# Ordering a split block's 24 products as three sweeps over its eight tiles

## The reference

```
h = rms_norm(x, g)          # [256, 1024]
proj = h @ w_in             # weights 1024 x (some thousands)
...
x = x + m @ w_out
```

## Time and profile before

| | |
|---|---|
| median of 3 runs | 1797.45 us (1797.22 to 1798.41) |
| the profiled execution | 1802.54 us |
| its span, first to last instruction | 1800.7 us |
| TensorE busy | 93% of the span |
| VectorE busy | 55% |
| ScalarE busy | 36% |
| TensorE's mean granted clock | 0.947 of full |

### The profile page before, as it was taken

The page is one execution under the profiler, slowest core; times in us unless marked ns, Lnnn a source line. Parts: engine busy times, 40 slices in busy tenths (PEclk is TensorE's granted clock), DMA queues, the critical chain, the costliest instruction groups (busy, mean ns, idle before and its releaser), DMA issues. The chain is left out here.

```text
span 1800.7 us, 29177 instructions
## 1 busy us (share of the span) xinstructions
PE 1676.3 (93%) x11890; PEld 1530.6 (85%) x11890; DVE 988.1 (55%) x1658; ACT 651.5 (36%) x899; POOL 12.5 (1%) x16
## 2 busy tenths in 40 slices
PE   7989999889998999989878999999999978988998
PEld 6788889889998889889878998899899868986677
DVE  6798554755556689564644334434433435456534
ACT  4542435344444543335332222222222224245321
POOL 1000000000000000000000000000000000000000
PEclk9999999999998999999987999999999988789899
DMA  7432233445553442222333878887788754422122
GB/s 276 150 105 76 79 106 103 140 133 188 187 193 129 141 140 94 71 100 89 116 107 119 292 268 276 273 291 267 278 280 283 277 204 145 157 79 79 59 71 82
DMA packets 82034, 292.72 MB, mean 163 GB/s; under 512 B 9095, under 2 KB 11647, under 8 KB 81679
## 3 DMA queue, kind: packets, MB, share of 16 engines
q1 hardware_dynamic: 81791, 290.10, 47.0%
q10 hardware_dynamic: 144, 1.24, 0.2%
HBM read 290.22 MB, written 1.08 MB: 162 GB/s over the span
## 5 line engine op out<-in xcount | busy, mean ns | idle before, releaser
L266 PE MATMUL bank_P<-h_hi,weights_hi 128*128 128x256 f32 x1584 | 475.1, 300 | 37.7 <-DVE h_lo L1069 18.9
L268 PE MATMUL bank_P<-h_hi,ring_lo 128*128 128x256 f32 x1584 | 458.2, 289 | 0.0
L267 PE MATMUL bank_P<-h_lo,weights_hi 128*128 128x256 f32 x1584 | 457.7, 289 | 0.0
L371 DVE TENSOR_TENSOR ring_lo<-ring,weights_hi 128x1024 fp32r<-128x1024 f32 x245 | 298.3, 1224 | 260.3 <-ACT weights_hi L352 257.6
L266 PEld LDWEIGHTS bank_P<-h_hi,weights_hi 128*128 128x128 f32 x1584 | 311.6, 197 | 54.5 <-issue 26.9
L352 ACT ACTIVATE weights_hi<-ring 128x1024 fp32r<-128x1024 f32 x245 | 257.2, 1058 | 221.1 <-PE bank_P L268 183.6
L268 PEld LDWEIGHTS bank_P<-h_hi,ring_lo 128*128 128x128 f32 x1584 | 315.9, 199 | 0.0
L267 PEld LDWEIGHTS bank_P<-h_lo,weights_hi 128*128 128x128 f32 x1584 | 312.6, 197 | 1.7 <-issue 1.0
L1507 PEld LDWEIGHTS bank_P<-arena,ring 128*128 128x128 f32 x2048 | 238.2, 193 | 7.3 <-issue 1.6
L1507 PE MATMUL bank_P<-arena,ring 128*128 x2048 | 238.6, 276 | 1.3 <-DVE arena L1621 1.3
L1647 DVE TENSOR_TENSOR arena<-arena,bank_P 128x96 f32<-128x96 f32 x64 | 16.3, 254 | 170.2 <-ACT arena L1553 170.2
(11 more groups left out here) (403 smaller groups left out, 2400.3 us busy)
## 6 DMA issues: line engine op xcount, KB each, us to landing
ring<-stream SPq DMA_DIRECT2D x541, 512.0 KB, 3.9
cst<-consts SPq DMA_DIRECT2D x1, 1712.0 KB, 10.5
arena<-params ACTq DMA_DIRECT2D x1, 1211.0 KB, 7.1
arena<-x SPq DMA_DIRECT2D x1, 1024.0 KB, 5.1
arena<-bias_vec SPq DMA_DIRECT2D x8, 128.0 KB
out<-arena SPq DMA_DIRECT2D x2, 512.0 KB
arena<-params SPq DMA_DIRECT2D x2, 256.0 KB, 7.6
arena<-bias_vec SPq DMA_DIRECT2D x8, 64.0 KB
```

The source lines that it names most:

```text
L266: pe.matmul(out, hi, x_hi, start=start, stop=False, skip_group_check=True)
L267: pe.matmul(out, hi, x_lo, start=False, stop=False, skip_group_check=True)
L268: return pe.matmul(out, lo, x_hi, start=False, stop=stop, skip_group_check=True)
L371: v.tensor_tensor(env["ring_lo"][:, slot, :], env["ring"][:, slot, :], env["w_hi"][:, i % HIS, :].bitcast(F32), ALU.subtract).then_inc(sel ...
```

## The change

The products of a block are no longer made tile by tile. A new method `sweeps` makes high x high for all eight tiles, then high x low activation for all eight, then low x high activation for all eight. TensorE waits for the high part ahead of the first sweep and for the low part ahead of the third. Where the activation is new, it waits for `h_hi_q` in the first sweep and for `h_lo_q` in the second. The block before is released with the first matmul instead of the third. In the scan of the mixer section, where a block's matmuls are dealt out between other products, they are still dealt out three at a time. The five places that call it are alike; one of them is shown.

```diff
+    def sweeps(self, out, x_hi, x_lo, hi_ready=None, lo_ready=None):
+        slot, part = (self.first + self.n) % RING, self.splits % HIS
+        self.n += 1
+        self.splits += 1
+        hi = self.env["w_hi"][:, part, :].rearrange("p (k n) -> p k n", k=KD)
+        lo = self.env["ring_lo"][:, slot, :].rearrange("p (k n) -> p k n", k=KD)
+        pe = self.pe
+        pe.wait_ge(self.env["sem"]("blocks_hi_parts_written"), self.splits)
+        for k in range(KD):
+            if hi_ready and k % 2 == 0:
+                pe.wait_ge(*self.env["after"](*hi_ready(k // 2)))
+            o, start = out(k)
+            mm = pe.matmul(o, hi[:, k, :], x_hi(k), start=start, stop=False, skip_group_check=True)
+            if k == 0:
+                self.release(mm)
+                self.unreleased += 1
+            yield mm
+        for k in range(KD):
+            if lo_ready and k % 2 == 0:
+                pe.wait_ge(*self.env["after"](*lo_ready(k // 2)))
+            yield pe.matmul(out(k)[0], hi[:, k, :], x_lo(k), start=False, stop=False, skip_group_check=True)
+        pe.wait_ge(self.env["sem"]("blocks_lo_parts_written"), self.splits)
+        for k in range(KD):
+            yield pe.matmul(out(k)[0], lo[:, k, :], x_hi(k), start=False, stop=(k == KD - 1), skip_group_check=True)
...
         def project(bank, j, name=None):
 
-            hi, lo = blocks.split()
-            for k in range(KD):
-                if blocks.n == 1 and k % 2 == 0:
-                    pe.wait_ge(*after(f"h_lo_{k // 2}"))
-                mm = three_passes(pe, bank[:, j * T:(j + 1) * T], hi[:, k, :], lo[:, k, :], h_hi[:, k, :], h_lo[:, k, :],
-                                  k == 0, k == KD - 1)
-                if k == 0:
-                    blocks.release(mm)
-            blocks.unreleased += 1
+            waits = (lambda q: (f"h_hi_{q}",), lambda q: (f"h_lo_{q}",)) if blocks.n == 0 else ()
+            for mm in blocks.sweeps(lambda k: (bank[:, j * T:(j + 1) * T], k == 0), lambda k: h_hi[:, k, :], lambda k: h_lo[:, k, :],
+                                    *waits):
+                pass
             return mm
```

More of the change, by code:

```diff
@@ L807, in gate_stream @@
                 bank = bank_of[turn[0] % 2]
[L808 to L819 removed]
+                out = bank[:, (n % 2) * T:(n % 2 + 1) * T]
+                for i, mm in enumerate(blocks.sweeps(lambda k: (out, k == 0), lambda k: h_hi[:, k, :], lambda k: h_lo[:, k, :])):
+                    if i == 3 * KD - 1 and n % 2:
+                        turn[0] += 1
+                        mm.then_inc(*done("pe", f"p_gate_{n // 2}"))
+                    if i % 3 == 2:
+                        yield
         stream = gate_stream()
@@ L861, in tensor @@
             for j in range(2):
-                hi, lo = blocks.split()
-                for k in range(KD):
-                    if q + j == 0 and k % 2 == 0:
-                        pe.wait_ge(*after(f"m_lo_{k // 2}"))
-                    mm = three_passes(pe, bank[:, j * T:(j + 1) * T], hi[:, k, :], lo[:, k, :], h_hi[:, k, :], h_lo[:, k, :],
-                                      k == 0, k == KD - 1)
-                    if k == 0:
-                        blocks.release(mm)
-                blocks.unreleased += 1
+                waits = (lambda i: (f"m_hi_{i}",), lambda i: (f"m_lo_{i}",)) if q + j == 0 else ()
+                for mm in blocks.sweeps(lambda k: (bank[:, j * T:(j + 1) * T], k == 0), lambda k: h_hi[:, k, :],
+                                        lambda k: h_lo[:, k, :], *waits):
+                    pass
             mm.then_inc(*done("pe", f"p_x_{q}"))
@@ L1695, in up @@
             for i in range(2):
-                hi, lo = blocks.split()
-                for k in range(KD):
-                    if f + i == 0 and k % 2 == 0:
-                        pe.wait_ge(*after(f"h2_lo_{k // 2}", "mix0"))
-                    mm = three_passes(pe, bank[:, i * T:(i + 1) * T], hi[:, k, :], lo[:, k, :], h_hi[:, k, :], h_lo[:, k, :],
-                                      k == 0, k == KD - 1)
-                    if k == 0:
-                        blocks.release(mm)
-                blocks.unreleased += 1
+                waits = (lambda q: (f"h2_hi_{q}", "mix0"), lambda q: (f"h2_lo_{q}", "mix0")) if f + i == 0 else ()
+                for mm in blocks.sweeps(lambda k: (bank[:, i * T:(i + 1) * T], k == 0), lambda k: h_hi[:, k, :],
+                                        lambda k: h_lo[:, k, :], *waits):
+                    pass
             mm.then_inc(*done("pe", f"tile_{f}"))
@@ L1956, in tile @@
         def tile(bank, j, waits=None):
-            hi, lo = blocks.split()
-            for k in range(KD):
-                if waits and k % 2 == 0:
-                    pe.wait_ge(*after(f"{waits}_{k // 2}"))
-                mm = three_passes(pe, bank[:, j * T:(j + 1) * T], hi[:, k, :], lo[:, k, :], h_hi[:, k, :], h_lo[:, k, :],
-                                  k == 0, k == KD - 1)
-                if k == 0:
-                    blocks.release(mm)
-            blocks.unreleased += 1
+            ready = (lambda q: (f"{waits}_hi_{q}",), lambda q: (f"{waits}_lo_{q}",)) if waits else ()
+            for mm in blocks.sweeps(lambda k: (bank[:, j * T:(j + 1) * T], k == 0), lambda k: h_hi[:, k, :], lambda k: h_lo[:, k, :],
+                                    *ready):
+                pass
             return mm
@@ L1990, in big @@
             mm.then_inc(*done("pe", name))
-        big("p_kvc", "vc_raw", (lambda b, j: tile(b, j, "h_lo"), tile))
+        big("p_kvc", "vc_raw", (lambda b, j: tile(b, j, "h"), tile))
         big("p_q0", "q0", (tile, tile))
@@ L2173, in tensor @@
         for i in range(4):
[L2174 removed]
+            big(f"p_x_{i}", f"x_{i}", (lambda b, j: tile(b, j, None if i else "m"), tile))
         for a in range(TT2):
```

13 lines of the change are left out of this document (removed).

## The result

The changed kernel took 1804.62 us in the median of 11 runs (1798.97 to 1808.48), the kernel before 1798.23 us in 11 runs on the same chip (1794.68 to 1801.62): a ratio of 1.0034, 95% interval 1.0022 to 1.0045, or 6.1 us more. A second set of 10 runs gave 1804.91 us and 1.0032 (1.0017 to 1.0046). The change made the kernel slower by a third of a per cent. The forecast was 1800.2 us in a range of 1795 to 1806, so the time lies in the range, but 4.4 us above the forecast, outside the forecast's own narrower range of 1797 to 1801, and nearer to rival (c) at 1806.

What follows compares the result with a forecast made beforehand. TensorE, busy for 93% of the span, was taken as the bound. Terms -5.1 + 5.9 + 2.0 = +2.8 us on 1797.45 us gave 1800.2 us; range 1795 to 1806, the forecast's own 1797 to 1801.

Steps and rivals of the forecast that it cites:

- rival (c): In the mixers' m blocks the clock falls behind a longer stop: +8.8 us, 1806 us, slower; chance 0.34.
- late wait at `conv_b`: At the first conv_b block, only DVE's wait for swap_q is won, in both layers: -5.1 us.
- h blocks: Four h blocks: six more matmuls behind the last high quarter, clock returning later in two: +5.9 us.
- m blocks: Three m blocks: six more matmuls behind the last high quarter, 0.65 us each: +2.0 us.
- distance inside a block: Matmuls inside a block were taken to stay 0.12 us apart at full clock; no cost counted.
- release with the first matmul: Release of the block before comes 0.24 us earlier and could hurry ACT's next high part; counted at nothing.
- the part that had 0.35: Chance given to the whole kernel being slower by over 0.2% (3.6 us).
- signs of being wrong: DVE idle between swap_q and squares, low clock behind the m blocks, or a distance other than 0.12 us inside the sweeps.
- The lower bound that I gave for a low clock in the block: At conv_b, with the clock low from 107.73 on as before, a layer gives 1.3 instead of 2.5 us.
- Rival (a): Waits at face value: all waits on the weight's low part go, -10.3 us, 1787.1 us, faster; chance 0.09.
- Rival (d): Each second use of a high tile costs the difference between load and distance: 131 us, 1929 us; chance 0.01.

Runs made afterwards that it cites:

- run 7: Kernel before with sweeps and late wait only in three blocks of each mixer section (two conv_b, first gate block), old release: 1792.68 us, 0.9961 to the kernel before.
- run 2: Changed kernel with the old tile order kept in the seven new-activation blocks (four h, three m): 1791.61 us, 0.9957 to the kernel before.
- run 4: As run 2, but the wait for the low part stands ahead of the block's first matmul: 1798.07 us, 0.9997 to the kernel before.
- run 10: Changed kernel with the four h blocks kept in the old tile order: 1796.41 us, 0.9991 to the kernel before.
- run 9: Changed kernel with the three m blocks kept in the old tile order: 1802.03 us, 1.0018 to the kernel before.
- run 5: Kernel before with only the release moved to the block's first matmul, order and waits old: 1796.78 us, 0.9984 to the kernel before.
- run 6: Changed kernel with the old release, at the third matmul: 1802.53 us, 1.0012 to the kernel before.
- run 8: Kernel before with early release everywhere, sweeps and late wait only in mixer blocks 16 to 26 and dense block 3: 1791.75 us, 0.9955.
- run 11: Changed kernel with weights_hi put ahead of the ring in SBUF, buffers between moved 12 KB a partition: 1792.29 us, 0.9967 to the kernel before.
- run 12: Changed kernel measured once more without any edit: 1804.91 us, 1.0032 to the kernel before.
- run 3: As run 2, but high x high and high x low of each tile together, only low x high as a sweep: 1792.94 us, 0.9968.
- run 1: Kernel before with sweeps only in the seven new-activation blocks (four h, three m): 1809.47 us, 1.0060 to the kernel before.

## Why the prediction was nearly right, and where it was not

| term | predicted, us | in the two traces | by the runs |
|---|---|---|---|
| late wait at `conv_b` | -5.1 | -4.5 | -7.0 (7), -7.2 (2 against 4) |
| h blocks | +5.9 | +5.9 | +7.7 (10) |
| m blocks | +2.0 | +4.9 | +2.9 (9) |
| distance inside a block | 0 | +3.7 | +2.3 (4 against 5) |
| release with the first matmul | 0 | not separable | -2.9 (5) |
| clock behind `p_q1`'s stop and near 1740 | 0 | -3.7 | not run |
| sum (in the traces with -0.3 of the dense section) | +2.8 | +6.0 | +3.0 |
| whole change | | +5.9 | +6.1 |

**What held and what did not.** That the kernel gets slower, why, and what the late wait and the h blocks do, held. But the change came out slower by more than the 3.6 us up to which the forecast gave itself 0.50, in the part that had 0.35, and two of the three things that were named as signs of being wrong came about: the clock fell in the m blocks, and the distance in the sweeps was another. That the time is in the range is in part luck: two terms that the sum had at nothing, +3.7 for the distance and -3.7 for the clock at two places, cancel in the traces.

**The late wait.** The argument held link by link: TensorE's 2.62 us stop turned into one of 1.99 us ahead of the 17th matmul, DVE's 2.53 us wait for `swap_q` vanished in layer 0 (9.67 us became 7.17), the stretch behind it kept its length, and the wait of TensorE for DVE at its end is still there, 2.50 us. The lower bound that I gave for a low clock in the block (1.3 instead of 2.5 us a layer) was approached in layer 1, where DVE still waits 0.68 us and the place gave 1.9. Rival (a) expected DVE's stretch to prove shorter than TensorE's; it did not. Yet the runs put the late wait at 7 us. In the traces of runs 4 and 2 the blocks from `conv_b` to the end of DVE's long stretch differ by less than 2 us in each mixer section, and the rest is stretches of low clock that are there in the one and not in the other, for one the stretch near 232. The changed kernel has it (length, busy times, clock):

```profile
230.00:236.00 6.00, 4.56 (x14) 3.81 (x15) 3.84 (x6) 1.91 (x2) 0.00 (x0) 0.72 0.00 0
```

Run 9 doesn't:

```profile
230.00:236.00 6.00, 3.33 (x16) 2.60 (x15) 5.32 (x10) 1.91 (x2) 0.00 (x0) 1.00 0.01 3
```

It is worth 1.5 us by the block ends. Whether such stretches account for all of the 2 us by which the runs exceed my term was not settled.

The granted clock of the executions points the same way. Within one kernel a higher mean clock goes with a shorter time: in run 6 from 0.948 (1808.52 us) to 0.960 (1791.44 us), some 1.4 us for each 0.001. The median clock is 0.949 before, 0.950 and 0.949 in the two sets of the change, 0.954 in run 4, and 0.9575, 0.955 and 0.9545 in runs 2, 7 and 8. At run 6's figure the 0.006 of run 7 would be some 8 us, an estimate as large as its whole gain. So much of what the late wait gives may be time at full clock, and not only the wait; no run holds the clock fixed, and a stop that is gone can't be followed by the low level either, so the two are not told apart here. The loss of the whole change does not show in its mean clock, nor does the gain of run 11 (0.950), which is as fast as these three.

**The h blocks.** Right in the mechanism, and in size by the traces: 18 matmuls behind the last high quarter, the return of the clock later in layer 0 and in the dense section, at 29.67 instead of 25.60 in the first. Where the block runs wholly at the low level, the six matmuls were priced too low, at 0.12 us each: they took 1.3 us, of which the block behind gave 0.6 back in layer 1, and so 0.7 came out by luck. The Trainium skill ("TensorE: Matmul & The Clock Gate", Part 1: The HAM clock gate) has the number of slow matmuls change from run to run. These runs agree: the block behind layer 0's h block has some at the low level in the change (3.46 us long instead of 2.74) and in run 12 fewer (3.34 us).

**The m blocks.** The step that failed here is the term of the sum, which took 0.65 us for each and left the fall of the clock to rival (c). The order's own cost was right (0.61 to 0.62 us where the clock held), and so was (c)'s account of the stop, 1.95 us between matmuls; only that it happens. In the changed kernel it did, in both places and in both traces, for 3 us. As the runs show, a stop of the same length is followed by either level, so a forecast could at best give it a chance, and (c) had 0.34. The time, +6.1 us, is between the forecast's +2.8 and (c)'s +8.8, on (c)'s side of the +3.6 us that divide them, though the four h blocks lost no more than forecast in the traces.

**The distance.** My last sentence named it as what could make the prediction wrong, "a distance other than 0.12 us inside the sweeps", and I had read it too coarsely: 0.12 stands for 117.7 ns before, and for 119.4 to 120.0 ns in the first two sweeps after (117.4 in the third, which takes its weights from the ring). The 0.034 us a block that follow from it are below what I looked at. Rival (d) sought the cause in the second use of a tile and priced it at 131 us; run 3 shows that this isn't it, run 4 that the late wait isn't, run 5 that the early release isn't, and run 11 that the place of the buffers is a part of it.

**The release.** "I count nothing for it" was wrong by 2.9 us in the kernel before (run 5, 1.3 to 4.5). In the change, run 6 has the opposite sign. `p_q1`'s block was at the low level in three of the four traces with the old release (4.34 us before and in run 1, 4.35 in run 7, but 2.83 in run 6), and at full clock in all ten with the early one but run 5's (3.84 us); so the 1.8 us there may be the release's. The 1.9 us near 1740 are not: run 1, with the old release, has 1.6 of them behind the same stop as before (1.48 us). The sum of the parts by the runs, +3.0 us, is 3 us short of the whole, about what the two clock falls in the m blocks cost, which the changed kernel has and runs 1 and 6 have not. That fits, but no run changed the fall alone, and the intervals of the parts, some 2 us each, allow for it without any cause; so it is argued and not shown.

## What to carry to other kernels

In a block whose activation is still being made, keep the order in which each tile's products are finished together; sweeps put six more matmuls behind the last piece, and in some traces the clock fell behind the pauses that they leave (the seven blocks cost 10.8 us in run 1, in whose trace the m blocks kept it). Wait late only where the profile shows that the early wait held up someone who then was late himself: six blocks of 213 gave 7.0 us (0.9961), and the late wait in 23 blocks with the early release 0.9955, the lowest here, though not clear of 0.9957 and 0.9961. Then read the distance of matmuls to the nanosecond, since a program of 11,890 of them multiplies it: moving one buffer in SBUF, and with it those behind it, made the changed kernel 12 us faster (run 11), and this was not tried together with the best order. And compare medians of many executions: a single trace of each kernel can differ by 3 us in a stretch that no edit touches.

## What the runs showed of the hardware

The distance of two 128x256 matmuls, each with its own weight load, has several levels at the full clock. From the same code they are 119.2 ns in the mean of a block with the high weights behind the ring (2.742 us over 23), 117.8 with `weights_hi` in front and the other buffers moved by 12 KB a partition (2.709), and 113.3 in some sections of that kernel (2.607). The old order in the old place has 117.7. The Trainium skill ("TensorE: Matmul & The Clock Gate", Step-by-step: what each phase is for) says that loading the next weights takes no read bandwidth from the running matmul; no run here tests that: run 11 shows that the place of the buffers changes the distance, and not whether it does so by the reads of TensorE or by ACT's and DVE's work on the same buffers. Which of the buffers that run 11 moved is the one that matters, and what the old order would gain from the move, stayed open.

A stop's length alone doesn't decide the clock behind it. In `p_q1` one of 2.27 us before the change was followed by the low level, one of 2.22 us in run 6 was not; in the m blocks one of 1.95 us was in the change and not in runs 1, 6 and 11. At the first `conv_b` block an idle time of 2.62 us was followed by the low level before (block of 4.22 us), one of 2.63 us in run 5 was not (2.79 us). Single executions of one kernel lie up to 17.1 us apart (run 6), more than any term of this study, so that no term here could be read from one run's time.
